# Attention with every matmul in two 64-row tiles: weighings beside scores, projections in halves

## The reference

```python
x = x + mixer_stick_breaking(rmsnorm(x, a_norm), a_w_in, a_w_out)      # then rmsnorm(x, final_norm)
# in the mixer:
q, k, v, g = jnp.split(jnp.einsum('bsd,de->bse', h, w_in), 4, axis=-1)
z = jnp.einsum('bthd,bshd->bhts', q, k) * scale                        # s < t only
after = lax.cumsum(log_rem, axis=3, reverse=True) - log_rem            # log_rem = log_sigmoid(-z)
w = jnp.where(mask, jnp.exp(log_beta + after), 0.0)                    # log_beta = log_sigmoid(z)
o = jnp.einsum('bhts,bshd->bthd', w, v)
out = jnp.einsum('bse,ed->bsd', o * jax.nn.silu(g), w_out)
```

## Time and profile before

| | us |
|---|---|
| runs | 1605.66, 1601.46, 1605.23; median 1605.23 |
| profiled execution | 1601.61 |
| its span | 1599.9 |
| PE, DVE, ACT, POOL busy | 1577.8, 1281.8, 848.4, 423.5 |
| first turns of slot 0, and of slot 158 | at 233.4 and 1411.9 |

### The profile page before, as it was taken

How to read it: one execution, slowest core, us unless ns; L and a number is a source line. 1 busy time by engine, 2 the same in 40 slices (tenths; PEclk the granted TensorE clock), 3 DMA queues, 4 the chain that set the end, 5 groups by cost and what they waited for, 6 DMA issues and landing times.

```text
span 1599.9 us, 34375 instructions
## 1 busy us (share of the span) xinstructions
PE 1577.8 (99%) x13762; PEld 1382.1 (86%) x13762; DVE 1281.8 (80%) x1525; ACT 848.4 (53%) x1558; POOL 423.5 (26%) x520
## 2 busy tenths in 40 slices
PE   9999999999999999999999999999999999999998
PEld 7888888888898888888888888888888988778887
DVE  5445439898889898898989898889899888967883
ACT  6535335555555556556556565565556555752221
POOL 0022034223323243323432433233223432000000
PEclk9999999999999999999999999999999999999999
DMA  9868654443434252435343443424243433879632
GB/s 304 268 182 271 203 159 126 125 124 99 137 102 136 74 158 78 139 86 146 110 115 115 120 117 96 138 91 143 77 142 103 131 110 110 326 254 342 206 106 79
DMA packets 205887, 237.82 MB, mean 149 GB/s; under 512 B 54560, under 2 KB 162080, under 8 KB 205728
## 3 DMA queue, kind: packets, MB, share of 16 engines
q1 hardware_dynamic: 113344, 160.30, 32.7%
q10 hardware_dynamic: 92384, 75.33, 15.3%
HBM read 155.78 MB, written 79.76 MB: 147 GB/s over the span
## 4 chain that ended last, share of the span: by engine, by line
PE 84%; DVE 9%; ACT 3%; issue 2%; DMA 1%; SPq 0%; DVEq 0%; ACTq 0%
PE z_ps L864 29%; PE z_ps L886 12%; PE o_ps L965 6%; PE turn_ps L919 6%; PE o_ps L964 6%; DVE u L1381 5%; PE turn_ps L995 5%; PE z_ps L817 5%; PE z_ps L995 4%; DVE r_turned_lo L1385 3%; PE o_ps L817 3%; PE turn_ps L817 3%; PE turn_ps L864 1%; PE turn_ps L886 1%; PE o_ps L995 1%
## 5 line engine op out<-in xcount | busy, mean ns | idle before, releaser
L1381 DVE TENSOR_TENSOR_SCAN u<-u,u 128x512 f32<-128x512 f32 x384 | 500.0, 1337 | 0.0
L1161 ACT ACTIVATE u<-z_ps 128x512 f32<-128x512 f32 (+3 forms) x593 | 288.1, 541 | 302.2 <-PE z_ps L886 301.7
L864 PE MATMUL z_ps<-hT_hi,w_hi 128*128 128x256 f32 x1472 | 432.5, 294 | 2.9 <-ACT u L1161 2.1
L1385 DVE TENSOR_TENSOR r_turned_lo<-turn_ps,r_turned_hi 128x1024 fp32r<-128x1024 f32 (+1 forms) x320 | 324.0, 1053 | 129.5 <-ACT r_turned_hi L1166 128.3
L864 PE MATMUL z_ps<-hT_hi,w_lo 128*128 128x256 f32 x1472 | 416.0, 283 | 0.0
L864 PE MATMUL z_ps<-hT_lo,w_hi 128*128 128x256 f32 x1472 | 415.9, 283 | 0.0
L864 PEld LDWEIGHTS z_ps<-hT_hi,w_hi 128*128 128x128 f32 x1472 | 280.6, 191 | 28.9 <-issue 17.5
L864 PEld LDWEIGHTS z_ps<-hT_lo,w_hi 128*128 128x128 f32 x1472 | 281.3, 191 | 0.0
L864 PEld LDWEIGHTS z_ps<-hT_hi,w_lo 128*128 128x128 f32 x1472 | 281.2, 191 | 0.0
L1166 ACT ACTIVATE r_turned_hi<-turn_ps 128x1024 fp32r<-128x1024 f32 (+1 forms) x320 | 270.5, 905 | 6.6 <-PE turn_ps L919 6.6
L759 POOL TENSOR_SCALAR w_raw<-w_raw,a_norm_col 128x128 f32<-128x128 f32 x192 | 171.4, 909 | 241.5 <-DMA w_raw<-in_w_qkg 241.5
(11 more groups left out here) (157 smaller groups left out, 2220.9 us busy)
## 6 DMA issues: line engine op xcount, KB each, us to landing
qk_hi_cols<-made ACTq DMA_DIRECT2D x128, 128.0 KB, 2.3
qk_lo_cols<-made ACTq DMA_DIRECT2D x128, 128.0 KB, 2.3
k_hi_twice<-qk_hi_cols SPq DMA_DIRECT2D x128, 128.0 KB, 3.4
k_lo_twice<-qk_lo_cols SPq DMA_DIRECT2D x128, 128.0 KB, 3.7
x_T<-in_xT SPq DMA_DIRECT2D x29, 512.0 KB, 6.3
w_raw<-in_w_qkg SPq DMA_DIRECT2D x24, 512.0 KB, 3.8
x_rows<-in_x SPq DMA_DIRECT2D x16, 512.0 KB, 5.2
v_rows<-v_stage ACTq DMA_DIRECT2D x32, 256.0 KB
```

Source lines behind the costliest of these rows:

```text
L864: last = nc.tensor.matmul(bank_of(g)[:, 0:GW], a[t % 2][:, k, :], b[:, c // 2, k, cols], start=(n == 0), stop=(n == QPM - 1))
L1161: nc.scalar.activation(u_t[(m // CB) % RU][r][:, 0:w], score_bank(m), ACT.Sigmoid, scale=-Z_SCALE).then_inc(s_u, 1)
L1381: nc.vector.tensor_tensor_scan(u, u, other, start, ALU.mult, op).then_inc(s_r, 1)
L1385: nc.vector.tensor_tensor(by_halves(rt_lo[p % 2][:], p), turned(p), by_halves(as_f32(rt_hi[p % 2][:]), p), ALU.subtract).then_inc(s_lo, 1)
```

## The change

Weighings and projections are issued as two matmuls of 64 rows each, so that PE has only 64-row matmuls from slot 0 to slot 159 (but for `put_out`). A half slot h is now the unit: turns of one pair, and two calls of `weigh_beside`, with `group_pairs` behind each.
- `weigh_beside` issues the four half weighings of a pair in one row tile, and between them the three score products of one step in the other; then, in the tile that has fewer columns, as many halves of projection matmuls as fit in the difference (one per 256 columns).
- Slot s weighs pair 2s - 1 (lower, then upper tile) in its first half and pair 2s (upper, then lower) in its second.
- `group_pairs` issues the upper half of a projection matmul and the lower half of one 30 places (`BEHIND`) earlier in the stream; they lie in different banks. `QUOTA` gives 12 places per half slot in diagonal slots, 15 in others; the stream of 178 groups ends in half slot 311.
- Scores use two banks, groups three; turns one double bank instead of two, so turns wait for `lo` of the pair ahead (`s_lo`). A weighing in the second tile waits until those of the first are done (`s_wu`, `s_wl`), since both add to `o_ps`; a group's lower half waits for its upper (`s_gu`).
- ACT and DVE go by half slots as well, with a group's evacuation at the start of the half slot after the one in which it ends, and scans one pair later.
- Dates that depend on these (weights, output weights, pieces of the output stage) move; the last pieces are due 8 steps earlier.

```diff
+AHEAD = {-2: (BEFORE, BEFORE + 1), -1: (BEFORE + 2, BEFORE + 3)}
+FIRST = BEFORE + 4
+BEHIND = 30
+QUOTA = {True: 12, False: 15}
+STREAM = (NG - FIRST) * QPM
...
+def limits():
+
+    upto = [0]
+    for h in range(2 * NU):
+        _, c, j, _ = STEPS[CB * (h // 2)]
+        upto.append(min(upto[-1] + QUOTA[c == j], STREAM + BEHIND))
+    return upto
...
-        turn_ps = [ctx.enter_context(nc.psum_tensor(f"turn_ps{n}", [P, 2, CH], F32)) for n in range(2)]
-        t_ps = [turn_ps[n // 2][:, n % 2, :] for n in range(4)]
+        turn_ps = ctx.enter_context(nc.psum_tensor("turn_ps", [P, 2, CH], F32))
+        t_ps = [turn_ps[:, 0, :], turn_ps[:, 1, :], pb("group_ps0"), pb("group_ps1")]
+        g_ps = [z_ps[2], t_ps[2], t_ps[3]]
...
+                def group_half(low):
+
+                    i = made_so_far[low]
+                    made_so_far[low] += 1
+                    g, n = FIRST + i // QPM, i % QPM
+                    t, c = GROUPS[g]
+                    cols = slice(c % 2 * GW, (c % 2 + 1) * GW)
+                    if n == 0 and low:
+                        pe.wait_ge(s_gu, g - FIRST + 1)
+                    if n == 0 and not low:
+                        pe.wait_ge(s_plo, g - 2)
+                        if g == FIRST_G[t]:
+                            pe.wait_ge(s_wlo, t + 1)
+                    rows = slice(low * HALF, (low + 1) * HALF)
+                    k, (a, b) = n // 3, ((w_hi, hT_hi), (w_hi, hT_lo), (w_lo, hT_hi))[n % 3]
+                    last = nc.tensor.matmul(bank_of(g)[:, 0:GW], a[t % 2][rows, k, :], b[rows, c // 2, k, cols],
+                                            start=(n == 0 and not low), stop=(n == QPM - 1 and low == 1))
+                    if n == QPM - 1:
+                        last.then_inc(s_p if low else s_gu, 1)
...
+                def left(h, low):
+
+                    limit = UPTO[h + 1] - BEHIND if low else UPTO[h + 1]
+                    return max(0, min(limit, STREAM) - made_so_far[low])
+
+                def group_pairs(h, share):
+
+                    both = min(left(h, 0), left(h, 1)) // share
+                    for _ in range(both):
+                        group_half(0)
+                        group_half(1)
+                    if share == 1:
+                        for low in range(2):
+                            for _ in range(left(h, low)):
+                                group_half(low)
...
+                def weigh_half(m, low, part):
+
                     h, c, j, r = STEPS[m]
-                    w = turn_width(m)
-                    if c == 0 and r == 0:
+                    w, p = turn_width(m), m // PAIR
+                    begin, end = j == c and r == 0, j == NC - 1 and r == CB - 1
+                    if c == 0 and r == 0 and part == 0:
                         pe.wait_ge(s_dlo, NC * h + j + 1)
-                    begin, end = j == c and r == 0, j == NC - 1 and r == CB - 1
-                    if begin and NC * h + c:
+                    first = begin and not low and part == 0
+                    if first and NC * h + c:
                         pe.wait_ge(s_ost, NC * h + c)
-                    p = m // PAIR
-                    if m % PAIR == 0:
+                    rows = slice(low * HALF, (low + 1) * HALF)
+                    here = slice(blocks_before(m) * P, blocks_before(m) * P + w)
+                    turned_part = (rt_hi, rt_lo)[part]
+                    last = nc.tensor.matmul(o_ps[:, 0:w], dv_head[rows, j * CB + sigma_block(m), :], turned_part[p % 2][rows, here],
+                                            start=first, stop=(end and not low and part == 1))
+                    if part == 1 and m % PAIR == 1:
+                        if p % 2 == 0 and not low:
+                            last.then_inc(s_wu, 1)
+                        elif p % 2 and low:
+                            last.then_inc(s_wl, 1)
+                        elif p % 2 and end:
+                            last.then_inc(s_o, 1)
+                        elif p % 2 and j == c:
+                            last.then_inc(s_dvused, 1)
+
+                def weigh_beside(p, low, m, h):
+
+                    weighed = inside(p // 2)
+                    scored = m < NS
+                    if weighed:
                         pe.wait_ge(s_lo, p + 1)
-                    here = slice(blocks_before(m) * P, blocks_before(m) * P + w)
-                    weights = dv_head[:, j * CB + sigma_block(m), :]
-                    nc.tensor.matmul(o_ps[:, 0:w], weights, rt_hi[p % 2][:, here], start=begin, stop=False)
-                    last = nc.tensor.matmul(o_ps[:, 0:w], weights, rt_lo[p % 2][:, here], start=False, stop=end)
-                    if end:
-                        last.then_inc(s_o, 1)
-                    elif j == c and r == CB - 1:
-                        last.then_inc(s_dvused, 1)
+                        if p % 2 == 0 and low:
+                            pe.wait_ge(s_wu, p // 2 + 1)
+                        if p % 2 and not low:
+                            pe.wait_ge(s_wl, p // 2 + 1)
+                    for i in range(2 * PAIR):
+                        if weighed:
+                            weigh_half(PAIR * p + i // 2, low, i % 2)
+                        if scored and i < 3:
+                            score(m, i)
+                    width = 2 * (turn_width(PAIR * p) + turn_width(PAIR * p + 1)) if weighed else 0
+                    spare = width - (3 * (CH - score_cols(m)) if scored else 0)
+                    idle = low if spare < 0 else 1 - low
+                    for _ in range(min(abs(spare) // GW, left(h, idle))):
+                        group_half(idle)
...
-                for s in range(-LEAD, NU):
-                    if inside(s + LEAD):
-                        scores_first(s + LEAD)
-                        if diagonal(s + LEAD):
-                            scores_second(s + LEAD)
+                for s in range(-LEAD, 0):
+                    pe.wait_ge(s_plo, BEFORE)
+                    score_pair(CB * (s + LEAD))
                     if s == -1:
                         pe.wait_ge(s_vT, 1)
-                    if s == 0:
-                        pe.wait_ge(s_plo, SLOT_GROUPS[-1][-1] + 1)
-                    if inside(s):
-                        pe.wait_ge(s_r, CB * s + CB)
-                        turns(2 * s)
-                        if skewed(s):
-                            turns_beside_scores(s)
-                        else:
-                            turns(2 * s + 1)
-                    if inside(s + LEAD) and not diagonal(s + LEAD) and not skewed(s):
-                        scores_second(s + LEAD)
-                    for n, g in enumerate(SLOT_GROUPS.get(s, [])):
-                        if s < 0:
-                            pe.wait_ge(s_plo, g - 3)
-                        elif inside(s + LEAD):
-                            pe.wait_ge(s_u, CB * (s + LEAD) + (3 if n else 1 if diagonal(s + LEAD) else 2))
-                        project(g)
+                    project(AHEAD[s][0])
+                    score_pair(CB * (s + LEAD) + PAIR)
+                    project(AHEAD[s][1])
+                pe.wait_ge(s_plo, FIRST - 2)
+                for s in range(NU):
+                    ahead = CB * (s + LEAD)
+                    pe.wait_ge(s_r, CB * s + CB)
+                    turns(2 * s)
+                    weigh_beside(2 * s - 1, 1, ahead, 2 * s)
+                    group_pairs(2 * s, 2)
+                    weigh_beside(2 * s - 1, 0, ahead + 1, 2 * s)
+                    group_pairs(2 * s, 1)
                     if s >= OUT_SLOT:
-                        put_out((s - OUT_SLOT) * QPM, (s - OUT_SLOT + 1) * QPM)
-                    if inside(s):
-                        for m in range(CB * s, CB * s + CB):
-                            weigh(m)
+                        put_out((s - OUT_SLOT) * QPM, (s - OUT_SLOT) * QPM + QPM // 2)
+                    turns(2 * s + 1)
...
                 for s in range(-LEAD, LAST_SLOT + 1):
-                    if inside(s):
-                        lo(2 * s)
-                        lo(2 * s + 1)
-                    here = SLOT_GROUPS.get(s, [])
...
+                    for part in range(2):
+                        h, first = 2 * s + part, CB * s + PAIR * part
+                        for g in finished(h - 1):
+                            made_low(g)
+                        if inside(s):
+                            lo(h)
+                        for m in range(first + LEAD_SCORES - PAIR, first + LEAD_SCORES):
+                            if 0 <= m < NS:
+                                scan(m)
+                        if s in AHEAD:
+                            made_low(AHEAD[s][part])
```

216 lines of the change are left out of this document (86 added, 130 removed).

## The result

The changed kernel takes **1629.18 us** (median of 4 runs, 1624.73 to 1635.98), the kernel before 1604.99 (4 runs): ratio 1.0159, 95% interval 1.012 to 1.0198. It is slower by 24 us. The forecast was 1632. The profiled execution is the longest of the four, 1635.98 us.

A forecast was written before the change was run, and what follows sets the result against it. PE passing its own list was taken to bound the kernel: 1601.6 us profiled, plus 20 for the longer list (blocking's 54 included) and 10 for waits, gave 1632. Range 8 in 10: 1570 to 1660; the forecast's own 1612 to 1660.

The forecast's parts named there:

- What bounds the kernel before: Attention stage: PE, busy 99%, passing its own list; start-to-start distances summed to 1158.5 us against 1178.5 in the trace.
- Removed switches, 72 us: PE's changes between 64-row and 128-row matmuls disappear: 160 x 0.45 us saved.
- blocking: Calls ahead of diagonal slots: one tile stands empty while its fills queue behind the other's fourth weighing; 54 us.
- Nothing is won from packing: PE matmuls: a 64-row half of 256 columns takes as long as the whole did, and scores were already paired.
- Hold-up in diagonal scores, 13 us: Diagonal scores: 256- and 128-column steps no longer wait for another's bank, saving about 4 x 0.2 us per head.
- Taking it that matmuls start in program order: Calls on PE: each matmul starts no earlier than the one ahead and its tile being free; 1632 us, without it 1578.
- Rival 1: Row tiles do not hold each other up, so the 54 us fall away: 1578 us; chance 0.31.
- the rule: Trainium skill's TensorE page: matmuls are strict FIFO without reordering, only weight loads going ahead; by it the sum is 1632.
- Waits, 10 us: PE waiting at turns for DVE's low part and at groups for evacuations: 10 us, between 0 and the earlier kernel's 20.
- does not bound: DVE's work in the attention stage: 1101 us, 69 a head against PE's 76.6, so DVE is not the limit.
- Rival 4: Turns or groups wait 0.15 us in each of 320 half slots: 48 us, 1670; within 0.08 for the slower two rivals.
- less 8 for the last slots with nothing to fill: End of the attention stage: 8 us taken off the stage's sum, which came to 1205 us.

The follow-up runs named there:

- experiment 6: Changed kernel with weighings whole over 128 rows once per half slot, scores in pairs, groups still in halves: 1673.73 us.
- experiment 1: Changed kernel with each call's projection fills spread between the weighings instead of all behind the fourth: 1631.39 us.
- Experiment 3: Changed kernel with ACT's copy that empties a finished chunk's output bank moved ahead, between the two sticks of the half slot: 1614.02 us.
- experiments 5: Changed kernel with DVE's low part made for half of its columns only from the seventh pair on, leaving out part of the product: 1602.05 us.
- 12: Kernel of 11 with DVE's low parts taking half of their columns, so part of the product is left out: 1577.97 us.
- experiment 9: Kernel of 8 with ACT's high parts of the two weights loaded before slot 0 taken 9 steps after their load instead of 5: 1604.1 us.
- 8: Kernel of Experiment 3 with most leftover projection pairs of a chunk-ending half slot moved behind the chunk's last weighings: 1604.24 us.
- 10: Kernel of 8 with 273 projection places per head instead of 276, three fewer in diagonal half slots: 1602.5 us.
- 11: Kernel of 8 with the edits of experiment 9 and 10, and fills spread as in experiment 1: 1602.0 us.
- experiment 2: Changed kernel with all four half weighings of a call issued first, then the three scores, then the fills: 1665.63 us.
- experiment 7: Kernel of Experiment 3 with ACT and DVE copying out the turned pair ahead of a finished group's evacuation: 1690.6 us.

## Why the number was right and the reason wrong

- **What bounds the kernel before**, distances and their sum: the distances held. In long runs of fills a pair of halves starts 0.118 us behind the one in front (0.12 in the forecast).
- **Removed switches, 72 us**: the prices were right, by experiment 6 (0.20 and 0.23 where 0.20 and 0.25 were read). But little of the 72 us reaches the list: PE's slots at their shortest, less the chunk waits of every head (1.2), go from 73.1 to 71.6 us a head, 24 us in all. The rest is in the forecast's own sum, which comes to 73.3 a head before (1158.5 / 15.8) and to 73.2 after without blocking: turns followed by matmuls twice as often, calls with one side narrower than the other. No run tested that by itself. What was missed is the trade: a longer list covers waits, and by experiment 6 about half of what is saved comes back as standing.
- **"Nothing is won from packing"**: fits, since both tiles' halves go at 0.23 and 0.12, but no run tested it alone. **Hold-up in diagonal scores, 13 us**: in the call shown above the 128-column products start 0.11 to 0.16 apart, without a stop.
- **"Taking it that matmuls start in program order"**: this step failed, 54 us. The timeline shows fills ahead of weighings, and experiment 1 finds nothing in the order. Rival 1, with 0.31, had the right mechanism; its 1578 is too low in the main by the waits, which it left at 10 us. The evidence that I held against it, that tiles of different pace "never need to overtake", said nothing either way, so the forecast hung on the rule alone.
- **Waits, 10 us, "between 0 and the 20"**: this failed in the other direction. By the starts of the waiting matmuls, PE stands in heads 1 to 14 about 23 us at turns, for the low part, 23 at the first weighing of a chunk, and 5 at group banks: 51 us. Some 17 of the chunk waits come in every head alike and lie inside the shortest slots. The forecast did the sum for `lo` ("ends about 2.7 to 4 us into a half slot that takes 3.2 to 4.5: hidden, with little left in the short ones"), and it was the short ones that counted. It never named the copy to `o_stage`, for which there is one bank: from the last weighing of a chunk to the first of the next PE has 1.3 to 2.1 us in the changed kernel, the waits included, and had 5.2 to 8.3 in the one before. Experiment 3 alone gave 15 us.
- **DVE "does not bound"** at 69 us a head against 76.6: right by load, wrong by effect. A part of it that ends late holds turns up, and experiments 5 and 12 put that at 27 and 24 us for half a low part.
- **Rival 4**, 48 us of waits and 1670, came closest in this term, but it stood on top of the blocking.
- **That the number came out is luck.** With its 10 us of waits the forecast has 77.2 us a head. For heads 1 to 14 that is 1081, against 1058.5 measured: 48 too many for blocking, 42 too few for waits, and about 17 too many in the rest of the list (6 of them by 0.12 instead of 0.118). Head 0 has 6 too few, and from head 15 to the end the forecast leaves 239, against 261.8: 23 too few. The errors cancel between the stretches as well as within them.
- **Start and end** were hardly costed ("less 8 for the last slots with nothing to fill"). Slot 0 starts 2 us earlier; head 0 is dearer in the profile by the stand and the clock of experiment 9. The end is 11 us longer in the changed kernel (250.6 to 261.8) although it has about 3 groups fewer to do, and 9 to 12 us longer in 3, 8, 9, 10 and 11 (259.9 in 11), so neither chunk waits nor quotas make it. Part of it is the clock, by the changed kernel's rows:

```profile
1380.00:1400.00 20.00, 18.96 (x269) 18.09 (x267) 16.82 (x19) 11.07 (x21) 0.74 (x1) 0.92 0.74 269
...
1420.00:1440.00 20.00, 16.89 (x174) 12.49 (x174) 19.46 (x22) 13.97 (x27) 0.00 (x0) 0.94 0.79 251
1440.00:1460.00 20.00, 19.40 (x104) 13.92 (x102) 10.24 (x15) 8.51 (x21) 0.00 (x0) 0.89 0.55 164
```

  What is missing there to a clock of 1.00 is 20 x (0.08 + 0.06 + 0.11) = 5 us at most. Another part is a stand at the start of head 15: ACT waits 3.06 us for the store of an earlier chunk before it can copy `o_ps`, and PE stands 3.7 us behind it (3.7 to 4.2 in 1, 3, 5, 6, 8 and 9, absent in 10 and 11).

```profile
1378.72 0.60 ACT L1190 ACTIVATE o_stage<-o_ps 128x512 f32<-128x512 f32 x1 [3.06 <-DMA o_lo_cols<-o_stage]
```

  The largest part is the weighings in halves themselves, once no scores and fills are left for the other tile. A pair in the last slots of the changed kernel, and behind it a slot (two pairs) of the kernel before:

```profile
1446.52 0.47 PE L957 MATMUL o_ps<-r_turned_hi,dv_head 64*128 64x512 f32 x1
...
1447.30 0.39 PE L957 MATMUL o_ps<-r_turned_lo,dv_head 64*128 64x512 f32 x1
1447.84 0.48 PE L957 MATMUL o_ps<-r_turned_hi,dv_head 64*128 64x512 f32 x1
...
1448.95 0.50 PE L1014 MATMUL z_ps<-wo_hi,gated_hi 128*128 128x512 f32 x1
```

```profile
1418.65 0.39 PE L964 MATMUL o_ps<-r_turned_hi,dv_head 128*128 128x512 f32 x1
...
1420.55 0.84 PE L919 MATMUL turn_ps<-ident,u 64*128 64x64 f32 x20
```

  A pair takes 2.43 us there, and two pairs took 1.90: the second tile's four halves wait for the first's (0.54 from 1447.30 to 1447.84, where 0.23 is the pace), and nothing runs beside either. From the turns of slot 158 to the last weighing, with the same 52 turns and 49 output products, it is 25.7 us against 16.1 before; experiment 6, with whole weighings, has 17.5. DVE at 19.46 of 20 us shows a further bound in the slots ahead of that; what it adds was not tried.

## What to carry to other kernels

When a list on the bounding engine gets shorter, first ask which waits it was covering: count for each shared buffer when its release comes, place by place, in the shortest stage and not in the mean. Here 72 us of saved switches left a list that was 24 us shorter, and it met 51 us of waits (in 14 heads) on a turn bank, an output bank and group banks, where the whole kernel before had 20; putting the copy that frees a bank first in its engine's order was worth 15 us, a few fills behind it 10. Work cut in halves pays only while the other half of the array has something to do: look at the last slots by themselves. And a forecast that comes out can rest on wrong terms that cancel: check the mechanism in the timeline before believing the number.

## What the hardware showed that was not expected

- Matmuls in two 64-row tiles overtake each other in time: a fill started at 660.12 ahead of weighings at 660.32 and 660.55 that the program issues before it, and in experiment 2 a score started with the weighing four places ahead of it (575.09).
- This isn't free without limit: in experiment 2 the overtaking tile lost 0.10 us once per call, of which one in a half slot shows in the time (4.06 us instead of 3.95), 36 us in all.
- After PE stood half of the time from 230 to 235 us, its granted clock read 0.62 in the next 5 us, so it had the lower of its two levels (1.2 of 2.4 GHz) for most of them, though PE was working again. In nine profiles with such a stand the clock fell in four and not in the other five, one of which (experiment 7) had PE busy for only 3.01 of the 5 us. Head 0 took 79.3 to 85.4 us with the fall and 75.3 to 79.6 without.
